# One kernel for two transformer blocks: the gate-scaled unit matrices made on GpSimd, a pair of slots per product, in place of ScalarE

## The chip, the cores and the metric

The kernel runs on one core of one Trainium2 chip. The metric is the device time of one launch in microseconds (us); the median of three runs is given. The core has five engines that run their own instruction streams and meet at semaphores: TensorE (PE; its weight loads are PEld), VectorE (DVE), ScalarE (ACT), GpSimd (POOL) and SyncE (SP). Sixteen DMA engines move data between HBM and SBUF for all of them.

## The reference

Two transformer blocks over 512 tokens of width 1024, in f32. Both end in the same kind of layer, a retrieval of single-neuron experts, and this layer fills nearly all of the kernel's time:

```
q = xn @ w_query;  s = q . sub_keys            # 8 heads, 2 halves, 128 keys
vals, idx = top_k(s, 16);  cand = vals0[:, None] + vals1[None, :]
best, pos = top_k(cand, 16)                    # expert = i1 * 128 + i2
gate = softmax(best)                           # 8 heads x 16 = 128 experts per token
a = einsum('cd,ced->ce', xb, u_tab[expert])    # one dot of 1024 per token and expert
w = gate * gelu(a)
out = einsum('ce,ced->cd', w, v_tab[expert])   # sum of 128 rows of v per token
```

Block 1 also has a state-space mixer and banded attention, block 2 compressed and selected attention and a short convolution.

## The kernel before

The 512 tokens are four tiles of 128 tokens, one token a partition; with two blocks that is n = 0 to 7. A tile has 128 experts per token, and each of them is a **slot**: s = 128 n + k, 1024 slots in all. For a slot

- GpSimd (`gpsimd_program`) issues an indirect DMA that gathers for each token one row of u and one of v (8 KB together, the table k_uv or k_vu by the ring's place) into `ring`, by the expert numbers in `idx`. The ring holds NU = 4 rows of u and NV = 8 of v, so gather s waits for dot s-4 and for product s-8 of TensorE.
- VectorE (`dot`) multiplies the u row with the token's xn and sums it into one column of `aw`.
- ScalarE (`weigh`, once for a pair of slots, PAIR = 2) applies gelu to two columns of `aw`, and makes for each slot `diag`, a 128x64 matrix with w on two stacked 64x64 diagonals: diag = gid * gelu(a).
- TensorE (`vmm`) multiplies `diag` with the v row and accumulates into two PSUM banks over the tile's 128 slots: four 64x64 products of 512 columns.

`gid` is `ident2` (two unit matrices of 64, one above the other) times the gate of the slot. It depends on no dot. ScalarE makes it for the next pair, right behind the two diag of this pair. `gid` and `diag` have four buffers, `s % (2 * PAIR)`, and `gate` has two, by tile.

Beside the slots of tile n the engines do the other work for tile n+1 (norm, projections, attention, routing, top-16). Each engine's program writes this out by hand: `place` gives for each part of a tile the slot at which it is due, and `pace` inserts the slots up to there (`slots`). The instructions of an engine run in this order. A `Lane` counts semaphores by stage, and `wait_ge(mark)` waits until the marked instruction is done. VectorE's `gates` writes the gates of head h of tile n after the top-16 of head h+1; for a later tile it first waits until the last gid that used the buffer is made. TensorE's weights come through SyncE's DMAs into `wsl`.

Of the kernel before, what the change touches and what calls it, by code (L numbers as in the profile page):

```python
# [8 lines left out]
ACT = mybir.ActivationFunctionType  # L9
# [10 lines left out]
NSLOT = 1024  # L20
PAIR = 2
# [78 lines left out]
def build(nc, A, out, act_counts):  # L100
    ctx = ExitStack()
    with ctx:
# [7 lines left out]
        def sb(name, shape, dt=F32):  # L110
            return ctx.enter_context(nc.sbuf_tensor(name, shape, dt))
# [12 lines left out]
        def bc(ap, shape):  # L124
            return ap.broadcast_to(shape)
# [18 lines left out]
        gate = sb("gate", [128, 2, 128])  # L144
        aw = sb("aw", [128, 2, 128])
        ident2 = sb("ident2", [128, 64])
        gid = sb("gid", [128, 2 * PAIR, 64])
        diag = sb("diag", [128, 2 * PAIR, 64])
# [170 lines left out]
        def u_at(s):  # L319
            return 3 * (s % NU) + 1  # L320

        def v_at(s):
            return 3 * (s % NU) + 2 * (s // NU % 2)
# [7 lines left out]
        def both_rows(s):  # L331
            at = min(u_at(s), v_at(s))
            return ring[:, at:at + 2, :].rearrange("p a b -> p (a b)")
# [16 lines left out]
        def shifted(copies, heads, a):  # L350

            return bass.AP(tensor=copies.tensor, offset=127 - 16 * a, ap=[[W1 - 1, 16], [16 * W1, heads], [1, 256]])
# [4 lines left out]
        def vector_program(v):  # L357
            V = Lane("v", v, sems, book)
# [58 lines left out]
            def ts(out, a_, s1, s2, o1, o2):  # L417
                if s2 is None:
                    return v.tensor_scalar(out, a_, s1, None, o1)  # L419
                return v.tensor_scalar(out, a_, s1, s2, o1, o2)  # L420

            def chained(inst_of, *marks):
                V.wait_own()
                V(inst_of(), *marks)
# [114 lines left out]
            def win1(n):  # L539
                for b in range(8):  # L540
                    pace(n, "win", b / 8)
                    if b < 6:
                        top(n - 1, b + 2, (n, "win", (2 * b + 0.7) / 16))
                    pace(n, "win", (2 * b + 1) / 16)
                    if b >= 4:
                        gate_logits(n, b)
                gates(n - 1, 7)
# [264 lines left out]
            def gates(n, h):  # L812
                R = RB[n // 4]
                V.stage("top")
                V.wait_ge("g_exp", n, h)
                if h == 0 and n >= 2:
                    V.wait_ge("gid", 128 * (n - 1) - 1)
                V(v.reciprocal(R["zs"][:, h:h + 1], R["zs"][:, h:h + 1]))
                chained(lambda: ts(gate[:, n % 2, 16 * h:16 * h + 16], R["best"][:, h, :], R["zs"][:, h:h + 1], None,
                                   ALU.mult, None), ("gate", n, h))  # L820

            def top(n, h, pause=None):
                R, b = RB[n // 4], n % 2
                vals, ixu, ixf, cand, best, pos = [R[k] for k in ("vals", "ixu", "ixf", "cand", "best", "pos")]
                pij, pf, oh, ee, nb = [R[k] for k in ("pij", "pf", "oh", "ee", "nb")]
                V.stage("top")
                if h == 0:
                    V.wait_ge("sS", n, 3)
                for k in range(2):
                    top16(R["halves"][h // 4][:, 2 * (h % 4) + k, :], R["s2"][:, 0:128], vals[:, k, :], ixu[:, k, :])  # L830
                chained(lambda: v.tensor_copy(ixf, ixu))
                V(tt(cand, bc(vals[:, 0, :].unsqueeze(2), [128, 16, 16]), bc(vals[:, 1, :].unsqueeze(1), [128, 16, 16]),
                     ALU.add))
                if pause:
                    pace(*pause)
                    V.stage("top")
                V.wait_own()
                top16(cand.rearrange("p a b -> p (a b)"), R["s2"], best[:, h, :], pos)
                V(ts(nb[:, h:h + 1], best[:, h, 0:1], -1.0, None, ALU.mult, None), ("g_nb", n, h))
                V.wait_own()  # L840
                V(ts(pij[:, 0, :], pos, 4, None, ALU.logical_shift_right, None))
                V(ts(pij[:, 1, :], pos, 15, None, ALU.bitwise_and, None))
                chained(lambda: v.tensor_copy(pf, pij))
                V.wait_ge("iot")
                chained(lambda: tt(oh, bc(pf.unsqueeze(3), [128, 2, 16, 16]), iob, ALU.is_equal))
                chained(lambda: tt(oh, oh, bc(ixf.unsqueeze(2), [128, 2, 16, 16]), ALU.mult))
                chained(lambda: v.tensor_reduce(ee, oh, AXX, ALU.add))
                chained(lambda: v.scalar_tensor_tensor(idx[:, b, 16 * h:16 * h + 16], ee[:, 0, :], 128.0, ee[:, 1, :],
                                                       ALU.mult, ALU.add), ("idx", n, h))
                if h:  # L850
                    gates(n, h - 1)
# [260 lines left out]
        def scalar_program(a):  # L1112
            S = Lane("a", a, sems, book)
            Q = Loads(S)

            def act(out, in_, f, **kw):
                return a.activation(out, in_, f, **kw)  # L1117

            def gated(s):

                n, k = divmod(s, 128)
                S.wait_ge("ident2")
                S.wait_ge("gate", n, k // 16)
                S(act(gid[:, s % (2 * PAIR), :], ident2[:, :], ACT.Copy, scale=gate[:, n % 2, k:k + 1]), ("gid", s))

            def weigh(g):

                n, k = divmod(PAIR * g, 128)
                sl = aw[:, n % 2, k:k + PAIR]
                S.stage("weigh")  # L1130
                if g == 0:
                    for j in range(PAIR):
                        gated(j)
                S.wait_ge("dot", PAIR * g + PAIR - 1)
                S(act(sl, sl, ACT.Gelu if n < 4 else ACT.Gelu_apprx_tanh), ("gelu", g))
                S.wait_own()
                for j in range(PAIR):
                    s = PAIR * g + j
                    if s >= 2 * PAIR:
                        S.wait_ge("vmm", s - 2 * PAIR)  # L1140
                    S(act(diag[:, s % (2 * PAIR), :], gid[:, s % (2 * PAIR), :], ACT.Copy, scale=sl[:, j:j + 1]), ("diag", s))
                if PAIR * g + PAIR < NSLOT:
                    for j in range(PAIR):
                        gated(PAIR * g + PAIR + j)

            def evacuate(n):
                S.stage("evac")
# [761 lines left out]
        def gpsimd_program(p):  # L1909
            G = Lane("p", p, sems, book)  # L1910
            Q = Loads(G)
            G.wait_ge("bias_lv", 0)
            lv = BB[0]["lv"][0:16, 0:W1]
            Q(p.dma_start(L1d, bc(lv.unsqueeze(1), [16, 16, W1])), "bias_d0", ("bias_d", 0))
            G.wait_ge("bias_lv", 1)
            lv = BB[1]["lv"][0:8, 0:W1]
            Q(p.dma_start(L2d, bc(lv.unsqueeze(1), [8, 16, W1])), "bias_d1", ("bias_d", 1))
            G.wait_ge("bias_d", 0)
            G.wait_ge("win", 0, 5)
            for a in range(8):  # L1920
                Q(p.dma_start(bias1[16 * a:16 * a + 16, :, :], shifted(L1d, 16, a)), "bias0",
                  *([("bias", 0)] if a == 7 else []))
            G.wait_ge("s_y", 0, 3)
            G.wait_ge("bias", 0)
            G.wait_ge("bias_d", 1)
            for s in range(NSLOT):
                n, k = divmod(s, 128)
                G.wait_ge("idx", n, k // 16)
                if s >= NU:
                    G.wait_ge("dot", s - NU)  # L1930
                if s >= NV:
                    G.wait_ge("vmm", s - NV)
                tab = A[("k_uv%d" if u_at(s) < v_at(s) else "k_vu%d") % (n // 4)]
                Q(p.indirect_dma_start(out=both_rows(s), out_offset=None, in_=tab,  # L1934
                                       in_offset=bass.IndirectOffsetOnAxis(ap=idx[:, n % 2, k:k + 1], axis=0)),
                  "ring%d" % (s % NU), ("fetch", s))
# [96 lines left out]
        for engines in ((Blank(),) * 5, (nc.vector, nc.scalar, nc.tensor, nc.gpsimd, nc.sync)):  # L2033
            vector_program(engines[0])
            scalar_program(engines[1])
            tensor_program(engines[2])
            gpsimd_program(engines[3])
            sync_program(engines[4])
            book.turn_over()
# [120 lines left out]
```

## Time and profile before

| what | value |
|---|---|
| median of three runs | 3590.83 us (3584.45 to 3600.45) |
| the profiled execution | 3584.01 us, span of its instructions 3582.6 us |
| busy: PE, PEld | 2508.1 us (70%), 984.3 us (27%) |
| busy: DVE, ACT, POOL | 2381.5 us (66%), 1369.2 us (38%), 1091.8 us (30%) |
| DMA | 1343.61 MB, mean 375 GB/s |

The span runs from the first instruction to the last. Busy time is that in which an engine executes; DMA issues of GpSimd (DMA_INDIRECT) count for it, its waits don't. The share of busy time is an average over stages, and an engine that is idle mostly waits for another one: the chain of waits and the list of waits say for whom.

### The profile page before, as it was taken

The numbers are of one execution on the slowest core, as the hardware profiler recorded it, in microseconds if no ns is written. First come the engines' busy times: TensorE is split into PE (matmuls) and PEld (weight loads), VectorE is DVE, ScalarE is ACT, GpSimd is POOL, SyncE is SP. The second block draws the span as 40 slices with busy tenths as digits, with TensorE's granted clock in tenths as the row PEclk, the third lists the DMA queues.
The fourth block names the chain that finished last, engine by engine and source line by source line (L and its number), as shares of the span: only waits on it lengthen the run. The fifth ranks groups of instructions, "written<-read, shape, count | busy, mean of one in ns | idle before, by whom it ended". The sixth has DMA issues, their size and how long they took to land.

```text
span 3582.6 us, 40111 instructions
## 1 busy us (share of the span) xinstructions
PE 2508.1 (70%) x13640; PEld 984.3 (27%) x13640; DVE 2381.5 (66%) x5690; ACT 1369.2 (38%) x3646; POOL 1091.8 (30%) x1038
## 2 busy tenths in 40 slices
PE   7767777686776867766667677767776778754555
PEld 3432332223322233222222233222332233211111
DVE  7448863688746887467664876568765877478444
ACT  1114332344323443133472427334563438333222
POOL 0002332223322233232332334332333333343332
PEclk9689788897798977888788888878888889877777
DMA  8659999999999999999999999999999999998998
GB/s 243 220 199 373 367 358 403 414 404 380 361 409 410 416 374 358 400 373 390 391 409 392 390 389 403 405 384 410 383 401 387 398 387 399 380 349 325 420 416 331
DMA packets 228013, 1343.61 MB, mean 375 GB/s; under 512 B 28360, under 2 KB 33768, under 8 KB 95968
## 3 DMA queue, kind: packets, MB, share of 16 engines
q0 software_dynamic: 148320, 1076.50, 75.4%
q1 hardware_dynamic: 78816, 262.43, 19.2%
q8 instruction: 107, 1.75, 0.2%
q10 hardware_dynamic: 672, 2.12, 0.1%
q14 instruction: 98, 0.80, 0.1%
HBM read 1338.24 MB, written 2.71 MB: 374 GB/s over the span
## 4 chain that ended last, share of the span: by engine, by line
DMA 33%; PE 29%; DVE 16%; issue 12%; POOL 4%; ACT 3%; SPq 0%; POOLq 0%; ACTq 0%; DVEq 0%
DMA ring<-in_k_uv,idx 17%; PE ps L1533 14%; DMA ring<-in_k_vu,idx 11%; PE ps L1462 10%; DVE ring L367 6%; DMA wsl<-in_k_wu 5%; POOL ring L1934 4%; PE ps L1671 1%; PE ps L1515 1%; ACT L1117 1%; DVE big L415 1%; PE ps L1617 1%; PE ps L1601 1%; PE ps L1775 1%; DVE pers L415 1%
## 5 line engine op out<-in xcount | busy, mean ns | idle before, releaser
L367 DVE CUSTOM_DVE_ANT_0 ring<-ring,xn 128x1024 f32<-128x1024 f32 x1024 | 1239.9, 1222 | 668.5 <-DMA ring<-in_k_uv,idx 358.7
L1462 PE MATMUL ps<-ring,diag 64*64 64x512 f32 x8192 | 1257.8, 736 | 498.9 <-ACT diag L1117 487.3
L1934 POOL DMA_INDIRECT ring<-in_k_vu,idx x512 | 541.8, 1058 | 1298.4 <-DVE aw L367 745.6
L1934 POOL DMA_INDIRECT ring<-in_k_uv,idx x512 | 544.0, 1062 | 1097.1 <-DVE aw L367 792.7
L1533 PE MATMUL ps<-wsl,xT 128*128 128x512 f32 (+1 forms) x1536 | 762.2, 644 | 162.6 <-DMA wsl<-in_k_wu 65.1
L1462 PEld LDWEIGHTS ps<-ring,diag 64*64 64x64 f32 x8192 | 305.4, 157 | 1218.8 <-ACT diag L1117 718.6
L1117 ACT ACTIVATE aw<-aw 128x2 f32<-128x2 f32 x512 | 103.9, 203 | 1227.8 <-DVE aw L367 1226.3
L1117 ACT ACT_TABLE_LOAD x373 | 478.6, 1283 | 54.4 <-DVE big L415 42.1
L1533 PEld LDWEIGHTS ps<-wsl,xT 128*128 128x128 f32 x1536 | 302.6, 207 | 624.5 <-issue 522.8
L1117 ACT ACTIVATE diag<-gid,aw 128x64 f32<-128x64 f32 x1024 | 306.1, 341 | 106.4 <-PE ps L1462 89.3
L1117 ACT ACTIVATE gid<-ident,gate 128x64 f32<-128x64 f32 x1024 | 292.5, 332 | 0.0
L1515 PE MATMUL ps<-ident,big 128*128 128x128 f32 x288 | 58.5, 325 | 93.7 <-ACT big L1117 51.1
L1671 PE MATMUL ps<-pers,rowB 128*128 128x64 f32 x224 | 50.1, 414 | 93.3 <-DVE rowB L673 69.9
L415 DVE TENSOR_TENSOR big<-ps,big 128x512 f32<-128x512 f32 x40 | 27.6, 690 | 99.4 <-PE ps L1533 99.1
L1515 PE MATMUL ps<-ident,xr 128*128 128x128 f32 x208 | 36.8, 332 | 68.4 <-DVE xr L419 46.4
L367 DVE DVE_READ_ACCUMULATOR2_ANT aw<- 128x1 f32 x1024 | 84.1, 82 | 0.0
L1117 ACT ACTIVATE xr<-ps 128x512 f32<-128x512 f32 x32 | 18.3, 589 | 169.1 <-PE ps L1533 165.5
L1515 PEld LDWEIGHTS ps<-ident,big 128*128 128x128 f32 x288 | 36.5, 160 | 151.6 <-ACT big L1117 77.6
L1671 PEld LDWEIGHTS ps<-pers,rowB 128*128 128x128 f32 x224 | 47.5, 321 | 104.9 <-issue 104.9
L802 DVE COPY xT<-ps 128x512 f32<-128x512 f32 x8 | 5.5, 691 | 102.3 <-PE ps L1515 102.3
L415 DVE TENSOR_TENSOR big<-big 128x512 f32<-128x512 f32 x84 | 58.1, 692 | 19.7 <-ACT big L1117 16.8
L1853 PE MATMUL ps<-pers,big 128*128 128x64 f32 x320 | 49.7, 292 | 27.2 <-DVE big L1013 27.2
(227 smaller groups left out, 2079.9 us busy)
## 6 DMA issues: line engine op xcount, KB each, us to landing
wsl<-in_k_wu SPq DMA_DIRECT2D x408, 512.0 KB, 10.9
wsl<-in_k_wmod SPq DMA_DIRECT2D x48, 512.0 KB, 9.7
ring<-in_k_vu,idx POOLq DMA_INDIRECT x512
ring<-in_k_uv,idx POOLq DMA_INDIRECT x512
wsl<-in_k_wu SPq DMA_DIRECT2D x16, 280.0 KB, 18.8
big<-in_b_gate SPq DMA_DIRECT2D x4, 1024.0 KB, 11.2
big<-in_conv_w SPq DMA_DIRECT2D x4, 768.0 KB, 23.9
hres<-in_x SPq DMA_DIRECT2D x4, 512.0 KB, 8.1
```

The costliest lines, as they stand in the source:

```text
L367: V(v.tensor_tensor_reduce(u_row(s), u_row(s), xn[:, b, :], 1.0, 0.0, ALU.mult, ALU.add, aw[:, b, k:k + 1]), ("dot", s))
L415: return v.tensor_tensor(out, a_, b_, op)
L1117: return a.activation(out, in_, f, **kw)
L1462: r = t.matmul(PA[half][64 * q:64 * q + 64, :], diag[64 * half:64 * half + 64, s % (2 * PAIR), :], v_row(s)[64 * half:64 * half + 64, 512 ...
L1515: r = t.transpose(PS[bank][:, j * 128:(j + 1) * 128], s_, ident[:, :])
L1533: r = t.matmul(PS[bank][:, 0:nn], lhsT(kk_), wsl[:, at % NWS, j, 0:nn], start=(kk_ == 0), stop=(kk_ == nk - 1))
L1601: x = t.matmul(PS[r // 2][:, 256 * (r % 2) + s0:256 * (r % 2) + 256], xT[64 * a_:64 * a_ + 64, 4 * m + r, :], kT1[64 * a_:64 * a_ + 64, m, ...
L1617: x = t.matmul(PS[2 + b][:, 256 * h + 128 * z:256 * h + 128 * z + 128], BT[32 * j:32 * j + 32, 4 * z + c, :], uT[32 * j:32 * j + 32, c, :] ...
L1671: x = t.matmul(PS[4 + h // 8][:, 64 * (h % 8):64 * (h % 8) + 64], PT1[:, r, 128 * k:128 * k + 128], v1[:, (n + 1 + k) % 2, 64 * g:64 * g + ...
L1775: r = t.matmul(PS[3 - isk][0:16, 0:64], blk_[:, isk, j, :], w1_[:, j, :], start=(j == 0), stop=(j == 31))
L1853: r = t.matmul(PS[4 + br][:, 64 * h:64 * h + 64], PT2[:, k % 2, 128 * j:128 * j + 128], vsn[:, j, 128 * br + 64 * g:128 * br + 64 * g + 64 ...
L1934: Q(p.indirect_dma_start(out=both_rows(s), out_offset=None, in_=tab, in_offset=bass.IndirectOffsetOnAxis(ap=idx[:, n % 2, k:k + 1], axis=0 ...
```

## The change

ScalarE no longer makes gid. GpSimd makes it with one product for a pair of slots: 128 partitions by 2 x 64 columns, `ident2` read twice, the two gates each read 64 times. The product for pair g stands in GpSimd's stream in front of the gather of slot 2g+4. It waits for the gates and for the second diag of pair g-2, which read the same two buffers. ScalarE's first diag of a pair now waits for it. Where GpSimd's stream ends, two products follow the last gather. VectorE's `gates` waits for the number of the pair instead of that of the slot.

```diff
--- before.py
+++ after.py
@@ -814,7 +814,7 @@
                 V.stage("top")
                 V.wait_ge("g_exp", n, h)
                 if h == 0 and n >= 2:
-                    V.wait_ge("gid", 128 * (n - 1) - 1)
+                    V.wait_ge("gid", 128 * (n - 1) // PAIR - 1)
                 V(v.reciprocal(R["zs"][:, h:h + 1], R["zs"][:, h:h + 1]))
                 chained(lambda: ts(gate[:, n % 2, 16 * h:16 * h + 16], R["best"][:, h, :], R["zs"][:, h:h + 1], None,
                                    ALU.mult, None), ("gate", n, h))
@@ -1116,32 +1116,20 @@
             def act(out, in_, f, **kw):
                 return a.activation(out, in_, f, **kw)
 
-            def gated(s):
-
-                n, k = divmod(s, 128)
-                S.wait_ge("ident2")
-                S.wait_ge("gate", n, k // 16)
-                S(act(gid[:, s % (2 * PAIR), :], ident2[:, :], ACT.Copy, scale=gate[:, n % 2, k:k + 1]), ("gid", s))
-
             def weigh(g):
 
                 n, k = divmod(PAIR * g, 128)
                 sl = aw[:, n % 2, k:k + PAIR]
                 S.stage("weigh")
-                if g == 0:
-                    for j in range(PAIR):
-                        gated(j)
                 S.wait_ge("dot", PAIR * g + PAIR - 1)
                 S(act(sl, sl, ACT.Gelu if n < 4 else ACT.Gelu_apprx_tanh), ("gelu", g))
                 S.wait_own()
+                S.wait_ge("gid", g)
                 for j in range(PAIR):
                     s = PAIR * g + j
                     if s >= 2 * PAIR:
                         S.wait_ge("vmm", s - 2 * PAIR)
                     S(act(diag[:, s % (2 * PAIR), :], gid[:, s % (2 * PAIR), :], ACT.Copy, scale=sl[:, j:j + 1]), ("diag", s))
-                if PAIR * g + PAIR < NSLOT:
-                    for j in range(PAIR):
-                        gated(PAIR * g + PAIR + j)
 
             def evacuate(n):
                 S.stage("evac")
@@ -1923,8 +1911,25 @@
             G.wait_ge("s_y", 0, 3)
             G.wait_ge("bias", 0)
             G.wait_ge("bias_d", 1)
-            for s in range(NSLOT):
+
+            def gated(g):
+
+                n, k = divmod(PAIR * g, 128)
+                G.stage("gid")
+                G.wait_ge("ident2")
+                G.wait_ge("gate", n, k // 16)
+                if g >= 2:
+                    G.wait_ge("diag", PAIR * (g - 2) + PAIR - 1)
+                j = g % 2 * PAIR
+                G(p.tensor_tensor(gid[:, j:j + PAIR, :], bc(ident2[:, :].unsqueeze(1), [128, PAIR, 64]),
+                                  bc(gate[:, n % 2, k:k + PAIR].unsqueeze(2), [128, PAIR, 64]), ALU.mult), ("gid", g))
+
+            for s in range(NSLOT + 2 * PAIR):
                 n, k = divmod(s, 128)
+                if s >= 2 * PAIR and s % PAIR == 0:
+                    gated(s // PAIR - 2)
+                if s >= NSLOT:
+                    continue
                 G.wait_ge("idx", n, k // 16)
                 if s >= NU:
                     G.wait_ge("dot", s - NU)
```

On GpSimd, in the first slots, each row is one kind of instruction with what it waits for (v_dot: the dots, t_vmm: TensorE's products, v_top: expert numbers and gates, a_weigh: ScalarE's gelu and diag). Before:

```order
L1934 DMA ring<-in_k_vu,idx 128x2048 [waits d_bias_d1,v_top,d_bias0,t_s5]
L1934 DMA ring<-in_k_vu,idx 128x2048 x3
L1934 DMA ring<-in_k_uv,idx 128x2048 [waits v_dot] x4
L1934 DMA ring<-in_k_vu,idx 128x2048 [waits t_vmm,v_dot] x4
L1934 DMA ring<-in_k_uv,idx 128x2048 [waits t_vmm,v_dot] x4
```

And after the change, the same slots:

```order
L1939 DMA ring<-in_k_vu,idx 128x2048 [waits d_bias_d1,v_top,d_bias0,t_s5]
L1939 DMA ring<-in_k_vu,idx 128x2048 x3
L1924 ISA
L1924 TENSOR_TENSOR gid<-ident,gate 128x128 [waits v_top,v_setup]
L1939 DMA ring<-in_k_uv,idx 128x2048 [waits v_dot] x2
L1924 TENSOR_TENSOR gid<-ident,gate 128x128
L1939 DMA ring<-in_k_uv,idx 128x2048 [waits v_dot] x2
L1924 TENSOR_TENSOR gid<-ident,gate 128x128 [waits a_weigh]
L1939 DMA ring<-in_k_vu,idx 128x2048 [waits t_vmm,v_dot] x2
L1924 TENSOR_TENSOR gid<-ident,gate 128x128 [waits a_weigh]
```

A product has come in front of every second gather, with a wait for ScalarE from the third one on; the gathers wait for what they waited for before.

On ScalarE, at its first two pairs (rowB<-rowB is the exp of the gates' softmax, aw<-aw the gelu). Before:

```order
L1117 ACTIVATE gid<-ident,gate 128x64 [waits v_setup]
L1117 ACTIVATE gid<-ident,gate 128x64
L1117 ACT_TABLE_LOAD
L1117 ACTIVATE aw<-aw 128x2 [waits v_dot]
L1117 ACTIVATE diag<-gid,aw 128x64 [waits a_weigh]
L1117 ACTIVATE diag<-gid,aw 128x64
L1117 ACTIVATE gid<-ident,gate 128x64 x2
L1117 ACT_TABLE_LOAD
L1117 ACTIVATE rowB<-rowB 128x16 [waits v_top]
```

And after the change:

```order
L1117 ACT_TABLE_LOAD
L1117 ACTIVATE aw<-aw 128x2 [waits v_dot]
L1117 ACTIVATE diag<-gid,aw 128x64 [waits p_gid,a_weigh]
L1117 ACTIVATE diag<-gid,aw 128x64
L1117 ACT_TABLE_LOAD
L1117 ACTIVATE rowB<-rowB 128x16 [waits v_top]
```

The two gid behind each pair of diag are gone, the first diag of a pair waits for GpSimd as well (p_gid), and the table loads stand where they stood.

## Rows read from the trace of the kernel before

**Rows 1.** The page: busy time, rate by slice, DMA in all, the gathers' queue.

```profile
span 3582.6 us, 40111 instructions
PE 2508.1 (70%) x13640; PEld 984.3 (27%) x13640; DVE 2381.5 (66%) x5690; ACT 1369.2 (38%) x3646; POOL 1091.8 (30%) x1038
...
DMA  8659999999999999999999999999999999998998
GB/s 243 220 199 373 367 358 403 414 404 380 361 409 410 416 374 358 400 373 390 391 409 392 390 389 403 405 384 410 383 401 387 398 387 399 380 349 325 420 416 331
DMA packets 228013, 1343.61 MB, mean 375 GB/s; under 512 B 28360, under 2 KB 33768, under 8 KB 95968
...
q0 software_dynamic: 148320, 1076.50, 75.4%
```

**Rows 2.** Windows: stretch, length, busy time by engine, clock, DMA share, GB/s.

```profile
290.00:1600.00 1310.00, 945.45 (x5256) 378.07 (x5255) 886.38 (x2000) 473.81 (x1297) 401.34 (x376) 0.84 0.97 387
1600.00:3300.00 1700.00, 1198.35 (x6643) 461.26 (x6641) 1202.62 (x3033) 776.17 (x1977) 583.76 (x543) 0.83 0.98 388
```

**Rows 3.** Timeline of VectorE's dots: start, length, idle time before, releaser.

```profile
1506.65 1.23 DVE L367 CUSTOM_DVE_ANT_0 ring<-ring,xn 128x1024 f32<-128x1024 f32 x1 [1.99 <-DMA ring<-in_k_uv,idx]
...
1510.39 1.22 DVE L367 CUSTOM_DVE_ANT_0 ring<-ring,xn 128x1024 f32<-128x1024 f32 x1 [2.51 <-DMA ring<-in_k_uv,idx]
...
1512.88 1.23 DVE L367 CUSTOM_DVE_ANT_0 ring<-ring,xn 128x1024 f32<-128x1024 f32 x1 [0.66 <-DMA ring<-in_k_uv,idx]
...
1515.36 1.23 DVE L367 CUSTOM_DVE_ANT_0 ring<-ring,xn 128x1024 f32<-128x1024 f32 x1 [1.24 <-DMA ring<-in_k_uv,idx]
```

**Rows 4.** The page: chain that ended last, by engine.

```profile
DMA 33%; PE 29%; DVE 16%; issue 12%; POOL 4%; ACT 3%; SPq 0%; POOLq 0%; ACTq 0%; DVEq 0%
```

**Rows 5.** Waits: who waited for whom, us in total, times, longest.

```profile
POOL ring L1934 <- DVE aw L367: 1538.3, 568, 37.0
ACT aw L1117 <- DVE aw L367: 1226.3, 341, 11.9
...
POOL ring L1934 <- PE ps L1462: 570.6, 224, 17.3
...
POOL ring L1934 <- issue: 105.2, 217, 3.6
```

**Rows 6.** The page's groups: busy us, mean ns, idle time before.

```profile
L367 DVE CUSTOM_DVE_ANT_0 ring<-ring,xn 128x1024 f32<-128x1024 f32 x1024 | 1239.9, 1222 | 668.5 <-DMA ring<-in_k_uv,idx 358.7
...
L1934 POOL DMA_INDIRECT ring<-in_k_uv,idx x512 | 544.0, 1062 | 1097.1 <-DVE aw L367 792.7
...
L1117 ACT ACT_TABLE_LOAD x373 | 478.6, 1283 | 54.4 <-DVE big L415 42.1
...
L1117 ACT ACTIVATE gid<-ident,gate 128x64 f32<-128x64 f32 x1024 | 292.5, 332 | 0.0
```

**Rows 7.** Products of two SBUF tiles on VectorE: timeline, then page's group.

```profile
1549.44 0.42 DVE L415 TENSOR_TENSOR rowB<-rowB 128x256 f32<-128x256 f32 x1
...
L415 DVE TENSOR_TENSOR big<-big 128x512 f32<-128x512 f32 x84 | 58.1, 692 | 19.7 <-ACT big L1117 16.8
```

**Rows 8.** Timeline of GpSimd's gathers; slots 4k to 4k+3 share a table.

```profile
1505.77 0.94 POOL L1934 DMA_INDIRECT ring<-in_k_uv,idx  x1 [0.30 <-issue]
1508.64 0.94 POOL L1934 DMA_INDIRECT ring<-in_k_vu,idx  x1 [1.94 <-DVE aw L367]
1511.89 0.94 POOL L1934 DMA_INDIRECT ring<-in_k_vu,idx  x1 [2.31 <-DVE aw L367]
1519.75 0.94 POOL L1934 DMA_INDIRECT ring<-in_k_vu,idx  x1 [6.92 <-DVE aw L367]
```

**Rows 9.** Timeline around slots 32 and 33.

```profile
397.18 1.35 POOL L1934 DMA_INDIRECT ring<-in_k_vu,idx  x1 [0.51 <-issue]
...
398.00 0.63 ACT L1117 ACTIVATE diag<-gid,aw 128x64 f32<-128x64 f32 x2
...
403.14 0.51 ACT L1117 ACTIVATE gt<-gt,cols 128x256 f32<-128x256 f32 x1 [2.73 <-DVE cols L419]
...
407.05 0.26 PEld L1462 LDWEIGHTS ps<-ring,diag 64*64 64x64 f32 x4 [0.43 <-issue]
```

## The prediction

> **What bounds the kernel now.** I read the page from the top: busy time, the slices, the DMA line. No compute engine is full, GpSimd least of all, but the DMA engines are busy 9 tenths or more in nearly every slice and move 375 GB/s over the span, 420 at best in a slice [rows 1]. All bytes at that best rate take 1343.61 MB / 420 GB/s = 3199 us, 89% of the span; in the two long stretches from 290 us to 3300 us, in which the slots run, it is 387 and 388 of 420 GB/s, 92% [rows 2]. A gather is 1076.50 MB / 1024 = 1.05 MB [rows 1], so 2.50 us at 420 GB/s, and where nothing disturbs it the dots start 2.48 us apart and wait for the gather [rows 3]. So the ring, four gathers deep, keeps the memory nearly full, and only some 8% of the slot stretch is there to be lost or won by the order of work on the engines. The chain of waits says the same: DMA 33%, PE 29%, DVE 16%, POOL 4%, ACT 3% [rows 4]. The list of waits tells who paces whom: GpSimd waits 1538.3 us for dots and 570.6 us for the products of TensorE before it may gather, and ScalarE waits 1226.3 us for dots in 341 of its 512 pairs [rows 5].
>
> **What is removed.** 1024 products gid of 332 ns in 292.5 us on ScalarE, two per pair, so 0.57 us each pair [rows 6]. ScalarE is busy 1369.2 us of the span [rows 1]. The two products stand behind diag and before the next gelu; where that gelu waits for a dot anyway they cost nothing. That holds in 341 of 512 pairs [rows 5]. In the other 171 something may have stood behind them: 171 x 0.57 = 97 us of ScalarE's time. How much of this reaches the end? The chain holds 3% of 3582.6 = 107 us of ScalarE's 1369.2, that is 0.08 of its busy time; 97 x 0.08 = **8 us gained**. The bound from above, all 97 on the path, would need a ScalarE that paces the rest, and the chain speaks against it. The 373 table loads [rows 6] stay, since the kind of function changes between gelu and the others as before, and a Copy asks for none.
>
> **What is added on GpSimd.** 512 products of 128x128 elements, one between an odd gather and the even one after it. Their duration d is on no row. From below: VectorE takes 0.42 us for such a product of 256 columns and 692 ns for 512 [rows 7], 1.06 ns a column, so 0.28 us for 128. From above: GpSimd's own gather, 1.06 us, and the 0.30 us that lie between two of its instructions [rows 6, 8], 1.36 us. I take d = 0.6 us, nearer the low end, as the product is small and the gather is the dearer kind of work. GpSimd gets 512 x 0.6 = 307 us more beside its 1091.8.
>
> Does it delay a gather? It stands in the queue ahead of the even gather and waits only for a diag of the pair two back, whereas the gather waits for a dot. So it runs while GpSimd sits idle. Between the gather at 1505.77 and that at 1508.64 there are 1.94 us, between 1511.89 and 1519.75 there are 6.92 us [rows 8]. The cover is gone only where gathers follow each other without a wait: 217 times [rows 5], half of them before an even one, 108. Each is later by d and one turn of 0.30 us: 108 x 0.9 = 97 us of GpSimd's time, of which by the chain (4% is 143 us of 1091.8, a share of 0.13) 13 us would reach the end. But then the odd gather has just been issued and keeps the memory busy for 2.50 us, and the even one follows after 0.94 + 0.30 + 0.9 = 2.14 us. So I take **0**, and keep 13 for the range. With a product over 1 us this cover begins to fail.
>
> **What is moved: the wait for gid.** diag of pair g now waits for GpSimd to have passed gather 2g+3 and the product. Gather 2g+3 needs the dot of slot 2g-1; diag of g needs the dot of 2g+1, two dots later, so two dots of 1222 ns [rows 6] even in the fastest run, 2.44 us, against 0.28 + 0.94 + 0.30 + 0.6 = 2.1 us (0.28 from the dot's end at 1511.61 to the gather at 1511.89 [rows 3, 8]). It can only come late where the gather waited for TensorE. The first such place: the gather of slot 35 runs from 397.18 for 1.35 us, and diag of slots 32 and 33 started at 398.00 [rows 9], so it would start at about 399.4, 1.4 us later; TensorE is then at earlier work and reaches slot 32 at 407.05 [rows 9]. What is late is hidden behind the 9 us that TensorE takes until it comes there. I take 0. Nothing else is queued behind the wait but ScalarE's own next instruction, an attention exp that waits until 403.14 [rows 9]. The first product of all needs the first gates, as gid does now.
>
> **What is added between the engines.** The new product reads SBUF from GpSimd, as the dot reads two operands from it on VectorE. Nothing on GpSimd reads a tile today, so no row shows whether they hold each other up. Below: nothing. Above: VectorE is held for all of d in each, 307 us. How often do they meet? Dots alone fill 1239.9 of some 3290 us, 38%; all of VectorE's work fills 886.38 + 1202.62 of 3010 us, 69% [rows 2, 6]. I take half: 256 meetings. In the example the product could start at 1506.71 and at 1512.83, and dots start at 1506.65 and 1512.88 [rows 3, 8]: the meeting is built into the rhythm, since the next dot starts about when the gather issue ends. If the one that comes first wins, VectorE loses on average half of d, 256 x 0.3 = 77 us. VectorE's share in the chain is 16%, 573 us of 2381.5 busy, 0.24; so 18 us at the end. Between 0 and 18 I take **9 us lost**.
>
> The Trainium skill, SBUF — State Buffer, section Who interferes with whom, speaks against the change here: a VectorE instruction with two SBUF inputs contends with a GpSimd instruction that reads SBUF, and whichever issues second blocks until the other is done. By that rule the term would be the upper one, 18 us, rather than 9; no row of the kernel before can show it, as its GpSimd reads no tile. The GPSIMD Engine Reference, section Performance versus the Vector engine, gives 4497 ns for a product of 2048 columns, so as an estimate about 0.3 us and a fixed part for 128; by that d would be under my 0.6 us.
>
> **Sum.** 3584.0 (the profiled execution, span 3582.6 and 1.4 around it) - 8 + 0 + 0 + 9 = 3585 us. The median of the runs is 3590.8, 6.8 above the profiled one, so **3592 us** as a median: no change that can be measured. (The three runs lie within 0.45%; about 0.5% is what a measurement can tell.)
>
> **Rivals.**
> *No measurable change (0.50)*: as above, 3574 to 3610.
> *Slower, VectorE is held (0.24)*: the dot or a product of the top-16 work waits for GpSimd's read. For it: the rhythm above, and VectorE's 69%. Against it: VectorE itself waits for the gather after a large part of its dots, so that a late dot eats its own idle time. With two products of three held for all of d: 341 x 0.6 = 205 us, x 0.24 = 49; 3592 - 9 + 49 = 3632 us. The price that decides between this and no change is VectorE's loss of about 110 us in all, 0.21 us for each product: 0.24 x 110 - 8 = 18 us, 0.5%.
> *Slower, GpSimd's queue is late (0.05)*: a pair of slots lasts 2 x 2.50 = 5.0 us when the memory is full. GpSimd needs 2 x 1.24 + d + 0.30, so it becomes the bound from d = 2.2 us. At 2.5 us it loses 0.3 x 512 = 150 us: 3740 us. The rows of VectorE and of GpSimd's own gather speak against such a d.
> *Faster, ScalarE was in the way (0.21)*: in the layers' attention and top-16 stages ScalarE changes between gelu and exp, and TensorE's transposes wait for it; 0.57 us earlier in the 171 places, with three of ten on the path: 29 us, and without the 8 and 9 us of the sum 3592 + 8 - 9 - 29 = 3562 us. For it: TensorE stands in program order, so a late diag blocks projections too. Against it: ACT is 3% of the chain, and the memory takes back what is gained.
>
> **How the numbers follow.** The likeliest is no change, so 3592. The range takes in most of the slower case (3632, with room above it) and part of the faster one (3562): 3555 to 3640; it leaves out about 0.07 below and 0.12 above. Faster by over 0.5%: 0.21; slower by over 0.5%: 0.24 + 0.05 = 0.29; within: 0.50.
>
> **What would show it.** In the profile after: gid on POOL x512, mean under 1 us, and ACT's busy time down by some 290 us to about 1080, with 373 table loads still. The page's GB/s unchanged near 375. The mean of the dot stays at 1222 ns if the engines don't hold each other, and grows if they do (by 0.08 us a dot for a loss of 77 us). The waits of PE for diag don't grow, and no long wait of ACT for gid appears. I am wrong if dots or the top-16 operations of VectorE grow by over 0.1 us each, if GpSimd's gathers start later behind the dot than 0.28 us in most slots, or if the rate of the slot stretch rises to 395 GB/s or more, which would mean that ScalarE's work did hold back the gathers.

## The result and the profile after

The changed kernel takes 3598.53 us in the median of 20 runs (3588.34 to 3607.49), the kernel before 3586.39 us in its 20 (3575.31 to 3600.45). The ratio is 1.0026, with a 95% interval of 1.0017 to 1.0035: 9.4 us slower (6 to 13), a small loss that the interval tells from nothing, and inside the half per cent that was called no change. The profiled execution took 3592.6 us with a span of 3591.1, against 3584.0 and 3582.6 before.

The page of the changed kernel, with the parts that answer to [rows 1], [rows 4] and [rows 6]:

```profile
span 3591.1 us, 39674 instructions
PE 2523.0 (70%) x13640; PEld 984.1 (27%) x13640; DVE 2420.9 (67%) x5690; ACT 1124.9 (31%) x2622; POOL 1406.5 (39%) x1550
...
DMA packets 228011, 1343.58 MB, mean 374 GB/s; under 512 B 28361, under 2 KB 33769, under 8 KB 95969
...
PE 28%; DMA 26%; DVE 17%; issue 16%; POOL 9%; ACT 3%; SPq 0%; POOLq 0%; ACTq 0%; DVEq 0%
...
L367 DVE CUSTOM_DVE_ANT_0 ring<-ring,xn 128x1024 f32<-128x1024 f32 x1024 | 1271.4, 1253 | 647.4 <-DMA ring<-in_k_uv,idx 356.9
...
L1117 ACT ACT_TABLE_LOAD x373 | 478.6, 1283 | 56.0 <-DVE big L415 43.8
...
L1924 POOL TENSOR_TENSOR gid<-ident,gate 128x128 f32<-128x128 f32 x512 | 271.3, 530 | 13.8 <-DVE gate L419 3.8
```

ScalarE lost 244.3 us of its 1369.2 us of busy time (its overlapping products of 292.5 us count for less there), and the end did not move with it. GpSimd gained 314.7 us. The reader should look at VectorE: nothing in its program changed, and it is busy 2420.9 us after 2381.5, 39.4 us more, of which the dots alone are 31.5, each 1253 ns on the mean after 1222. In the chain POOL went from 4% to 9%.

The list of waits of the changed kernel, for GpSimd and for ScalarE, against [rows 5]:

```profile
POOL ring L1939 <- DVE aw L367: 1417.8, 565, 32.9
ACT aw L1117 <- DVE aw L367: 1380.1, 346, 12.4
...
POOL ring L1939 <- PE ps L1450: 347.4, 133, 17.3
...
POOL ring L1939 <- issue: 74.8, 280, 7.7
```

ScalarE's time went into waiting for dots: 1380.1 us after 1226.3. GpSimd's added work came out of its waits, 1417.8 after 1538.3 and 347.4 after 570.6.

Where VectorE's 39 us come from stands in the timeline of GpSimd and VectorE. First a product that starts 0.28 us into a dot, then a dot that starts 0.01 us after a product has started, then a dot that starts 0.12 us after one, then a product beside an operation of the top-16 (a search, FIND_INDEX8):

```profile
519.76 0.94 POOL L1939 DMA_INDIRECT ring<-in_k_uv,idx  x1 [0.30 <-issue]
520.44 1.23 DVE L367 CUSTOM_DVE_ANT_0 ring<-ring,xn 128x1024 f32<-128x1024 f32 x1 [1.82 <-DMA ring<-in_k_vu,idx]
520.72 1.19 POOL L1924 TENSOR_TENSOR gid<-ident,gate 128x128 f32<-128x128 f32 x1
...
522.31 0.97 POOL L1939 DMA_INDIRECT ring<-in_k_uv,idx  x1 [0.39 <-issue]
...
1771.90 0.94 POOL L1939 DMA_INDIRECT ring<-in_k_vu,idx  x1 [1.42 <-DVE aw L367]
1772.87 0.41 POOL L1924 TENSOR_TENSOR gid<-ident,gate 128x128 f32<-128x128 f32 x1
1772.88 1.48 DVE L367 CUSTOM_DVE_ANT_0 ring<-ring,xn 128x1024 f32<-128x1024 f32 x1 [1.25 <-DMA ring<-in_k_vu,idx]
...
1715.39 0.41 POOL L1924 TENSOR_TENSOR gid<-ident,gate 128x128 f32<-128x128 f32 x1
1715.51 1.38 DVE L367 CUSTOM_DVE_ANT_0 ring<-ring,xn 128x1024 f32<-128x1024 f32 x1 [2.23 <-DMA ring<-in_k_uv,idx]
...
1542.51 0.41 POOL L1924 TENSOR_TENSOR gid<-ident,gate 128x128 f32<-128x128 f32 x1
1542.58 0.28 DVE L810 FIND_INDEX8 rowB<-rowB 128x8 uint32<-128x128 f32 x1
```

The first product lasts 1.19 us in place of 0.41 and ends 0.24 us after the dot does: the dot was first, the product waited, and the next gather went out late. The dot at 1772.88 takes 1.48 us in place of 1.22: here the product was first. The dot at 1715.51 takes 1.38. So a dot is not held to the product's end: 1.48 less 1.22 is 0.26 us where the product had 0.40 left, and 0.16 us where it had 0.29 left; both dots go on some 0.28 us after the product's start. In the last case both take what they take alone; the search reads one tile. So the two engines do hold each other up when GpSimd reads SBUF and the dot reads two tiles, and the rhythm that the prediction named (the next dot is due when the gather issue ends) is there to be seen at 1772.88.

The time of a product and who waits for it, from the answer on the tile gid:

```profile
L1924 POOL TENSOR_TENSOR gid<-ident,gate x512: 399/407/1509, 252.1 to 3568.6; 128x128 f32<-128x128 f32 x171
...
  POOL gid L1924: 21.3, 14
```

Undisturbed it is 407 ns, in the median; the mean of 530 holds the waits. Counted over the whole trace, 139 dots last over 1.30 us (none did before), some 34 us more in all, and 122 products last over 0.50 us, 63 us more in all. So the product waits as often as the dot does, and longer, and the gather behind it waits with it. ScalarE's diag waited for it 14 times, 21.3 us in all.

### The profile page after: what moved, and what is told of

Same layout as the page of the kernel before. It is cut to its first block, busy times and chain, and to the rows that moved or that the text cites. A ratio compares the mean times of both kernels' runs of the same rounds, so it can differ in the third digit from the quotient of the medians.

```text
span 3591.1 us, 39674 instructions
## 1 busy us (share of the span) xinstructions
PE 2523.0 (70%) x13640; PEld 984.1 (27%) x13640; DVE 2420.9 (67%) x5690; ACT 1124.9 (31%) x2622; POOL 1406.5 (39%) x1550
## 4 chain that ended last, share of the span: by engine, by line
PE 28%; DMA 26%; DVE 17%; issue 16%; POOL 9%; ACT 3%; SPq 0%; POOLq 0%; ACTq 0%; DVEq 0%
PE ps L1521 13%; DMA ring<-in_k_uv,idx 12%; DMA ring<-in_k_vu,idx 10%; PE ps L1450 9%; POOL ring L1939 7%; DVE ring L367 6%; DMA wsl<-in_k_wu 4%; POOL gid L1924 2%; DVE big L415 1%; ACT L1117 1%; PE ps L1659 1%; PE ps L1503 1%; PE ps L1605 1%; DVE rowB L415 1%; PE ps L1589 0%
## 5 line engine op out<-in xcount | busy, mean ns | idle before, releaser
L367 DVE CUSTOM_DVE_ANT_0 ring<-ring,xn 128x1024 f32<-128x1024 f32 x1024 | 1271.4, 1253 | 647.4 <-DMA ring<-in_k_uv,idx 356.9
L1939 POOL DMA_INDIRECT ring<-in_k_vu,idx x512 | 557.8, 1089 | 1141.2 <-DVE aw L367 698.3
L1939 POOL DMA_INDIRECT ring<-in_k_uv,idx x512 | 571.3, 1116 | 937.3 <-DVE aw L367 719.5
L1450 PEld LDWEIGHTS ps<-ring,diag 64*64 64x64 f32 x8192 | 306.4, 158 | 1228.3 <-ACT diag L1117 757.2
L1117 ACT ACTIVATE aw<-aw 128x2 f32<-128x2 f32 x512 | 104.0, 203 | 1381.5 <-DVE aw L367 1380.1
L1924 POOL TENSOR_TENSOR gid<-ident,gate 128x128 f32<-128x128 f32 x512 | 271.3, 530 | 13.8 <-DVE gate L419 3.8
```

Source lines behind the costliest of these rows:

```text
L367: V(v.tensor_tensor_reduce(u_row(s), u_row(s), xn[:, b, :], 1.0, 0.0, ALU.mult, ALU.add, aw[:, b, k:k + 1]), ("dot", s))
L1450: r = t.matmul(PA[half][64 * q:64 * q + 64, :], diag[64 * half:64 * half + 64, s % (2 * PAIR), :], v_row(s)[64 * half:64 * half + 64, 512 ...
L1924: G(p.tensor_tensor(gid[:, j:j + PAIR, :], bc(ident2[:, :].unsqueeze(1), [128, PAIR, 64]), bc(gate[:, n % 2, k:k + PAIR].unsqueeze(2), [12 ...
```

## Experiments

After the result there were two theories. **A**: the loss is the hold of VectorE, less a few us that ScalarE's relief gave back. **B**: the loss is the length of GpSimd's queue, gathers that go out later, and the hold costs nothing. C, beside them: ScalarE's relief is worth nothing. All ratios are to the kernel before on the same chip, with a 95% interval in brackets.

**e1: GpSimd's product alone.** The kernel before, with the product into a spare tile; ScalarE keeps gid.

```diff
+        gsp = sb("gsp", [128, 2 * PAIR, 64])
...
+                G(p.tensor_tensor(gsp[:, j:j + PAIR, :], bc(ident2[:, :].unsqueeze(1), [128, PAIR, 64]),
+                                  bc(gate[:, n % 2, k:k + PAIR].unsqueeze(2), [128, PAIR, 64]), ALU.mult), ("gsp", g))
```

> The kernel before, with GpSimd's product as in the change but into a spare tile that nobody reads; ScalarE still makes gid. Theory A (VectorE is held while GpSimd reads SBUF, and ScalarE's relief gave a few us back): the mean of the dot 1250 to 1255 ns again, and the ratio to before above that of the change, 1.004 to 1.006. Theory B (GpSimd's queue is late, the hold costs nothing): a ratio near that of the change too. Theory C (ScalarE's relief is worth nothing): 1.002 to 1.0035, the change's own loss, no more.

Measured: 1.0037 (1.0022 to 1.0051), dot mean 1254 ns. The ratio lies between what A and C expected and the interval reaches into both. The whole loss is made by what was added; taking the work from ScalarE changed it by 0.001, which the intervals don't tell from nothing.

**e2: ScalarE's relief alone.** The gates are left out.

```diff
-                    S(act(diag[:, s % (2 * PAIR), :], gid[:, s % (2 * PAIR), :], ACT.Copy, scale=sl[:, j:j + 1]), ("diag", s))
-                if PAIR * g + PAIR < NSLOT:
-                    for j in range(PAIR):
-                        gated(PAIR * g + PAIR + j)
+                    S(act(diag[:, s % (2 * PAIR), :], ident2[:, :], ACT.Copy, scale=sl[:, j:j + 1]), ("diag", s))
```

> The kernel before without gid: ScalarE's diag reads the unit matrices directly, so the gates are left out of the result; GpSimd has only its gathers. This is the relief of ScalarE alone, 292 us less work on it. As predicted for it, 8 us faster: ratio 0.998. Theory C, off the path: 0.9995 to 1.0005. If ScalarE had been in the way, 0.992 or less.

Measured: 0.9993 (0.9978 to 1.0008), 2.5 us faster, with an interval from 8 faster to 3 slower. The 8 us that were predicted lie at its edge; that the relief is worth nothing fits as well. Its page:

```profile
PE 2505.9 (70%) x13640; PEld 983.3 (27%) x13640; DVE 2382.8 (67%) x5690; ACT 1125.4 (31%) x2622; POOL 1095.8 (31%) x1038
```

ScalarE is at the changed kernel's 1125 us, the others where they were, and the time stands. ScalarE was not in the way: the bound set for that, 0.992, is far outside the interval.

**e3: a memset in place of the product.** It holds the place in the queue and the waits, and reads nothing; gid holds ones.

```diff
-                G(p.tensor_tensor(gid[:, j:j + PAIR, :], bc(ident2[:, :].unsqueeze(1), [128, PAIR, 64]),
-                                  bc(gate[:, n % 2, k:k + PAIR].unsqueeze(2), [128, PAIR, 64]), ALU.mult), ("gid", g))
+                G(p.memset(gid[:, j:j + PAIR, :], 1.0), ("gid", g))
```

> The changed kernel with a memset of the same 128x128 piece in place of the product, so gid holds ones and the result is not the reference's; GpSimd reads no tile now but keeps its place in the queue and its waits. Theory A: the mean of the dot goes back to 1222 to 1225 ns and the loss is gone, ratio 0.998 to 1.000. Theory B: the gathers are still behind an instruction, ratio 1.0015 to 1.003, unless the memset is far shorter than the product's 407 ns.

Measured: 1.0006 (0.9991 to 1.002). The groups of its page:

```profile
L367 DVE CUSTOM_DVE_ANT_0 ring<-ring,xn 128x1024 f32<-128x1024 f32 x1024 | 1240.4, 1222 | 681.2 <-DMA ring<-in_k_uv,idx 370.5
...
L1924 POOL MEMSET gid<- 128x128 f32 x512 | 113.8, 222 | 4.0 <-DVE gate L419 3.7
```

The dot is back at 1222 ns, so the reads make the hold of the dot. What is left of the loss is 2 us, with an interval from 3 gained to 7 lost. But the memset is also less than half as long as the product, and this run alone can't part A from B.

**e4: the product twice**, the second into the spare tile of e1.

```diff
                                   bc(gate[:, n % 2, k:k + PAIR].unsqueeze(2), [128, PAIR, 64]), ALU.mult), ("gid", g))
+                G(p.tensor_tensor(gsp[:, j:j + PAIR, :], bc(ident2[:, :].unsqueeze(1), [128, PAIR, 64]),
+                                  bc(gate[:, n % 2, k:k + PAIR].unsqueeze(2), [128, PAIR, 64]), ALU.mult), ("gsp", g))
```

> The changed kernel with the product made twice, the second time into a spare tile. Theory A: VectorE's busy time grows by another 35 to 45 us over the change (dot mean about 1280 ns), ratio 1.005 to 1.006. Theory B: the gap between gathers that follow each other grows by another 0.4 us, ratio also 1.004 to 1.006, with the dot near 1253 ns.

Measured: 1.0066 (1.0040 to 1.0091), dot mean 1268 ns, VectorE busy 2448.8 us. The ratio is just above what both theories named, and its interval covers both, so it can't part them. The dot's mean grew by 15 ns over the change, about half of what A expected, and VectorE's busy time by 27.9 us in place of 35 to 45.

**e5: a memset as long as the product.**

```diff
-        gid = sb("gid", [128, 2 * PAIR, 64])
+        gidl = sb("gidl", [128, 2, 416])
...
-                G(p.tensor_tensor(gid[:, j:j + PAIR, :], bc(ident2[:, :].unsqueeze(1), [128, PAIR, 64]),
-                                  bc(gate[:, n % 2, k:k + PAIR].unsqueeze(2), [128, PAIR, 64]), ALU.mult), ("gid", g))
+                G(p.memset(gidl[:, g % 2, :], 1.0), ("gid", g))
```

> The changed kernel with a memset of 128x416 ones in place of the product (the result is not the reference's): from the 222 ns of 128 columns and 0.1 us of one column I expect about 0.5 us, as long as the product lasted on the mean (530 ns), but GpSimd reads no tile. Theory A, the loss is VectorE's hold: dot mean 1222 ns and ratio 0.999 to 1.001, as for the short memset. Theory B, the loss is GpSimd's queue: ratio 1.002 to 1.0035, as for the change, with the dot at 1222 ns.

Measured: 1.0027 (1.0011 to 1.0044). The dots and GpSimd's memsets:

```profile
L367 DVE CUSTOM_DVE_ANT_0 ring<-ring,xn 128x1024 f32<-128x1024 f32 x1024 | 1240.2, 1221 | 682.6 <-DMA ring<-in_k_uv,idx 364.3 <-DMA ring<-in_k_vu,idx 312.3 <-issue 3.4
...
L1923 POOL MEMSET gidl<- 128x416 f32 x512 | 237.4, 464 | 4.0 <-DVE gate L419 3.7
```

The dot is not held, VectorE is busy only 2.4 us more than before, and the loss is that of the change. Theory A alone falls: 464 ns in front of every second gather cost something by themselves, 10 us (4 to 16) for 268.3 us more of GpSimd, 0.04 for each. This run alone would explain the whole loss of the change.

**e6: the product behind the wait for the dot.**

```diff
+                    if NU <= s < NSLOT:
+                        G.wait_ge("dot", s - NU)
                     gated(s // PAIR - 2)
```

> The changed kernel with the product behind the wait for the dot that the even gather waits for, and not before it. The product then starts 0.28 us after a dot's end, when VectorE often waits for the next rows, but the even gather is later by 0.4 us and a turn each time. Theory A: the dot's mean falls towards 1230 ns and the ratio is under the change's, 0.9995 to 1.002. Theory B: 256 or more gathers later by 0.7 us on the queue, ratio 1.004 or more.

Measured: 1.0079 (1.0062 to 1.0096), 28 us. The dot's mean fell to 1230 ns as A expected, and the time went the other way:

```profile
L1924 POOL TENSOR_TENSOR gid<-ident,gate 128x128 f32<-128x128 f32 x512 | 293.1, 573 | 787.9 <-DVE aw L367 763.7 <-PE ps L1450 21.3
```

Here the product always stands between the wait for a dot and the gather. In 343 of 512 places it sat idle for the dot itself (the list of waits), so there it made the gather late by its whole length; in others the gather then waited for something else. 28 us (22 to 34) reach the end, some 0.1 us for each of the products' 293.1 us, though the memory is nearly full. Of the places tried, this one in the queue is the dearest. What theory B had named, 1.004 or more, held.

**e7: a dose on VectorE**, in the kernel before.

```diff
+                if s >= 2:
+                    V.wait_ge("dose", s - 2)
+                V(v.tensor_copy(spare[:, s % 2, :], ident[:, 0:64]), ("dose", s))
```

> The kernel before with a copy of 128x64 on VectorE into a spare tile behind each dot; GpSimd and ScalarE as before. It measures what VectorE's time is worth at the end. I expect some 0.1 us each, 80 to 120 us in all, and by the share of the chain (0.24) 19 to 29 us: ratio 1.005 to 1.008. If the weight is that, the change's 39 us of VectorE give its 9 us and theory A needs nothing else. If the ratio is under 1.002, VectorE's time is worth little here, and the loss must come from GpSimd's queue.

Measured: 1.0054 (1.0034 to 1.0075), 19 us. From its page and its group:

```profile
PE 2511.9 (70%) x13640; PEld 982.9 (27%) x13640; DVE 2484.4 (69%) x6714; ACT 1368.5 (38%) x3646; POOL 1120.8 (31%) x1038
...
L372 DVE COPY spare<-ident 128x64 f32<-128x64 f32 x1024 | 193.8, 189 | 0.0
```

VectorE is busy 103.0 us more (the copies overlap the dots' ends), so 19.4 / 103.0 = 0.19 us at the end for each (0.12 to 0.26 by the interval). The price taken from the chain was 0.24. The gathers are not held by the copy itself: they still start 0.28 us after a dot's end.

**e8: four memsets as long as two products** (gid and three times 256 columns of a spare tile), the partner of e4.

```diff
+                G(p.memset(gid[:, j:j + PAIR, :], 1.0), ("gid", g))
+                if g:
+                    G.wait_ge("fill", g - 1)
+                for i in (0, 1, 0):
...
+                        G(p.memset(fill[:, 0, :], 1.0), ("fill", g))
+                    else:
+                        G(p.memset(fill[:, i, :], 1.0), ("fill%d" % i, g))
```

> The changed kernel with four memsets in place of the product, 128 columns of gid and three times 256 of a spare tile: about 1.2 us for each pair, as in the run with the product made twice, but GpSimd reads no tile (gid holds ones, so the result is not the reference's). Theory B, the loss is the length of GpSimd's queue alone: ratio 1.0055 to 1.0075, as for the doubled product, with the dot at 1222 ns. Theory A in part, the hold of VectorE (67 us in that run) has its own price of 0.19 for each us as the dose on VectorE gave, 13 us: ratio 1.002 to 1.004.

Measured: 1.0043 (1.0027 to 1.0059), between what the two theories expected, and its interval overlaps that of e4. GpSimd is busy 1617.9 us here and 1743.3 in e4, so the two are not of one length either. Inconclusive.

**e9: one product for four slots** (128x256, 256 of them).

```diff
-        gid = sb("gid", [128, 2 * PAIR, 64])
+        gid = sb("gid", [128, 4 * PAIR, 64])
...
-                if s >= 2 * PAIR and s % PAIR == 0:
-                    gated(s // PAIR - 2)
+                if s >= 2 * PAIR and s % (2 * PAIR) == 0:
+                    gated(s // (2 * PAIR) - 1)
```

> The changed kernel with one product for four slots (128x256, 256 of them, eight buffers of gid): about 0.7 us each, so GpSimd has 180 to 230 us of products in place of 271, and half as many chances to meet a dot. Both theories: less loss than the change, ratio 1.001 to 1.002. A ratio above 1.003 would mean that one long product in front of a gather costs more than two short ones.

Measured: 1.0036 (1.0020 to 1.0052), a miss: the loss is not shown to be less than that of the change, nor, by the interval, to be more. From its page and GpSimd's groups:

```profile
PE 2539.2 (70%) x13640; PEld 995.0 (28%) x13640; DVE 2429.5 (67%) x5690; ACT 1126.3 (31%) x2622; POOL 1319.7 (37%) x1294
...
L1924 POOL TENSOR_TENSOR gid<-ident,gate 128x256 f32<-128x256 f32 x256 | 188.0, 734 | 8.8 <-DVE gate L419 3.7
```

The products take 83 us less of GpSimd than in the change, but VectorE is busy 48.0 us more than before, not 39.4. Fewer and longer products did not hold it less.

**e10 and e11: a triple dose**, with reads and without. e10 makes the product three times; e11 has six memsets, 128 columns and five times 256. The lines of e11:

```diff
+                for i in range(5):
+                    if i >= 2:
+                        G.wait_ge("fill%d" % (i - 2), g)
+                    G(p.memset(fill[:, i % 2, :], 1.0), ("fill%d" % i, g), *([("fill", g)] if i == 4 else []))
```

> The changed kernel with the product made three times, twice into spare tiles: about 1.8 us of GpSimd for each pair, and VectorE held some 90 to 100 us in all. So far the losses fit two prices together: 0.15 to 0.19 for each us that VectorE is held, and about 0.02 to 0.03 for each us of GpSimd's queue. By both: 15 to 18 and 19 to 28 us, ratio 1.009 to 1.013. By the queue alone (theory B), the same ratio as the run with memsets of the same length.

> The changed kernel with six memsets in place of the product, 128 columns of gid and five times 256 of a spare tile, about 1.8 us for each pair, no tile read (gid holds ones, so the result is not the reference's). Both prices: without the hold 15 to 18 us less than the tripled product, ratio 1.005 to 1.008. Theory B: within 0.001 of the tripled product.

Measured: e10 1.0145 (1.0128 to 1.0163), e11 1.0086 (1.0069 to 1.0103), both a little above what the two prices gave, by less than their intervals. The page and the dots of e10, then those of e11:

```profile
PE 2534.4 (70%) x13640; PEld 994.4 (27%) x13640; DVE 2487.2 (68%) x5690; ACT 1125.0 (31%) x2622; POOL 1968.0 (54%) x2574
...
L369 DVE CUSTOM_DVE_ANT_0 ring<-ring,xn 128x1024 f32<-128x1024 f32 x1024 | 1302.9, 1284 | 649.3 <-DMA ring<-in_k_uv,idx 339.9 <-DMA ring<-in_k_vu,idx 303.2 <-issue 4.7
```

```profile
PE 2528.6 (70%) x13640; PEld 986.9 (27%) x13640; DVE 2420.2 (67%) x5690; ACT 1124.8 (31%) x2622; POOL 1870.3 (52%) x4110
...
L368 DVE CUSTOM_DVE_ANT_0 ring<-ring,xn 128x1024 f32<-128x1024 f32 x1024 | 1240.6, 1223 | 673.2 <-DMA ring<-in_k_uv,idx 365.9 <-DMA ring<-in_k_vu,idx 303.1 <-issue 1.5
```

The intervals don't meet. The difference, 0.0059 or 21 us, goes with 67.0 us of VectorE and 97.7 us of GpSimd, part of which is itself waiting for VectorE. At 0.04 for each, the 97.7 us of GpSimd would give 4 of the 21. Theory B alone falls as well: products that read cost more than memsets that fill the same queue. Which side of a meeting costs it, the dot that is held or the gather behind a product that is held, these two runs can't part. If all of the 21 us is the hold of VectorE, it costs 0.31 for each us; the dose of e7 says 0.19. And e11 costs 31 us with 778.5 us more of GpSimd, 0.04 for each us of queue, or 0.03 if the 38.7 us more of VectorE in it are first taken off at 0.19.

## Why the prediction was right, and where its terms were off

The time, 3598.5, is in the range and 6.5 us over the forecast of 3592; the forecast of no measurable change held by the bound given, but the sum of its terms (+1 us) was too small against 9.4 (6 to 13). Part of the closeness is luck. The forecast stands on the 3590.8 us of three runs of the kernel before, and 20 runs gave 3586.4, so that 4.4 us of the missing loss were in the starting point. And 8 us gained against 9 lost cancel each other, where the runs show some 2.5 gained and a loss that has a part in GpSimd's queue, which was put at 0.

*What bounds the kernel.* Right. The rate stayed (374 after 375 GB/s over the span, 388 and 385 in the two slot stretches after 387 and 388), and of the 314.7 us put on GpSimd and the 39.4 on VectorE only 9 us reached the end.

*ScalarE, 8 us gained.* e2 gives 2.5, with an interval from 8 gained to 3 lost, so the term stands at the upper edge. That it would be small was right, since ScalarE mostly waits for dots; the price of 0.08 was measured by nothing closer than this. The rival in which ScalarE was in the way falls with e2.

*The product's duration, 0.6 us.* 407 ns alone, 530 with its waits. The estimate from VectorE's rows, 0.28 us, was the nearer bound. The 4497 ns that the prediction quotes from the Trainium skill (GPSIMD Engine Reference, Performance versus the Vector engine) are those of an addition of 2048 columns, not of a product, 2.2 ns a column; the runs here show 1.7 ns for each further column and some 0.2 us beside it.

*GpSimd's queue, taken as 0 with 13 for the range.* This is the step that was mis-sized. The cover that was named, 2.50 us of transfer under the odd gather against 2.14 us, counted the gap of a back-to-back pair too high, and yet was not a full cover. In the changed kernel such a pair stands so:

```profile
1535.55 0.94 POOL L1939 DMA_INDIRECT ring<-in_k_uv,idx  x1 [0.30 <-issue]
1536.52 0.41 POOL L1924 TENSOR_TENSOR gid<-ident,gate 128x128 f32<-128x128 f32 x1
1537.08 0.97 POOL L1939 DMA_INDIRECT ring<-in_k_vu,idx  x1 [0.16 <-PE ps L1450]
```

1.53 us lie between the two gathers and not 2.14, against 1.24 without a product. Still e5, whose memset holds no dot, lost 10 us (4 to 16), and e11 31 us. A full cover would have given nothing in both. The term measured 10 us where 0 was taken, inside the 13 kept for the range. How a gather that is late by less than one transfer still costs time at the end was not traced to single places.

*The hold, 9 us between 0 and 18.* That the dots are held is shown by the rows above, and by e3 and e5, in which nothing reads and the dot is back at 1221 or 1222 ns. VectorE lost 39.4 us where 77 were reckoned. The number of meetings was guessed well (256, against 139 long dots and 122 long products), but in half of them it was the product that waited, and a held dot lost 0.25 us on the mean and not 0.3. At 0.19 to 0.31 for each us, 39.4 us would be 7 to 12 us; at the change's own dose no run shows such a share, since e5 lost as much without it. The trace agrees with the Trainium skill's rule (SBUF — State Buffer, Who interferes with whom) in who meets whom: a product that starts behind a dot waits for its end, a search with one input is not held (0.28 us), and memsets, which only write, leave the dot at 1221 to 1223 ns. It does not agree that the second blocks until the first is done: a dot right behind a product's start is held by 0.26 us of the 0.40 left. The rule makes no price at the end; e7 gives one for VectorE's time, and e10 against e11 one for the meetings.

*The wait for gid, 0.* Right: 14 waits, 21.3 us in all, on an engine that is idle for two thirds of the span. TensorE's weight loads waited 757.2 us for diag after 718.6, though the prediction had said that the waits for diag don't grow; what that costs no run shows.

*The signs of being wrong.* None appeared. The dot grew by 0.031 us and not by 0.1, most gathers still start 0.28 us after a dot's end, and the slot stretch stayed under 395 GB/s.

At these prices the parts would be 7 to 12 us for the hold, 9 to 13 for the queue (314.7 us more of GpSimd at 0.03 to 0.04) and 2.5 back, 14 to 22 us against 9.4 measured; so the prices, most of them taken at larger doses, don't simply add up at this one. That GpSimd's queue costs something without any read is shown by e5 and e11. That reads cost something beyond it is shown at three times the dose, by e10 against e11, and not for the change itself. How the 9.4 us divide is open. One rival was not tested: TensorE's granted clock, as a share of full speed, was 0.824 on the mean in the 20 runs of the changed kernel and 0.826 in the 29 runs of the kernel before beside e1 to e4, among which a clock lower by 0.01 goes with 10 us more. That would be some 2 of the 9.4 us; whether it is a cause or follows from the longer waits is not shown. No version tried beats the kernel before: e2, which makes no gid at all and leaves the gates out, is the best that moving it could reach, and its gain is not told from nothing.

## What to carry to other kernels

Work moved off an engine pays only if that engine is in the chain; ask the list of waits first (ScalarE waited for dots in 341 of 512 pairs) and try the removal alone (e2) before building the other side. GpSimd's idle time is not free where it issues the gathers: each us in its queue cost 0.03 to 0.04 us at the end when it stood ahead of a wait (e5, e11) and 0.1 when it stood behind one (e6). And a small read on GpSimd beside a VectorE that mostly reads two SBUF tiles takes VectorE's time too, here 31 us of dots for 512 products, and the product's own, 63 us.

## What the runs showed of the hardware

A memset on GpSimd, which leaves dots alone, holds other work of VectorE: small scalar operations from SBUF to SBUF. One group of e11, which was 162 ns on the mean before the change and 161 after it (its 64 of 128x16 alone are 171 ns in both and 409 in e11), and copies from PSUM, which last 482 ns in all three:

```profile
L420 DVE TENSOR_SCALAR pers<-pers 128x16 uint32<-128x16 uint32 (+2 forms) x97 | 20.1, 319 | 1.2
...
L1014 DVE COPY big<-ps 128x128 f32<-128x128 f32 (+3 forms) x32 | 15.4, 482 | 0.0
```

That is where most of e11's 38.7 us more of VectorE come from, with the dot at 1223 ns. The product itself is 407 ns for 128 columns and 622 ns in the median for 256 (e9): by these two, an estimate of 1.7 ns for each further column and some 0.2 us that any product costs.
